# Rank rows read back in pair layout inside the experts' stage, with shared rows and residual summed in its loop

## The reference, cut to what matters

```python
h = layer_norm(ALPHA * x + merged @ prm['w_out'], prm['ln1_g'], prm['ln1_b'], LN_EPS)
y = layer_norm(ALPHA * h + moe_ffn(h, prm), prm['ln2_g'], prm['ln2_b'], LN_EPS)
# moe_ffn: each token goes to TOP_K = 8 of N_EXPERTS = 128 experts, and to one shared expert
h = jax.nn.silu(xb @ prm['w_e1'][e]) * (xb @ prm['w_e3'][e])
yb = (h @ prm['w_e2'][e]).astype(jnp.float32) * w[:, None]
shared = (jax.nn.silu(xt @ prm['w_s1']) * (xt @ prm['w_s3'])) @ prm['w_s2']
return (shared.astype(jnp.float32) + routed).astype(x.dtype).reshape(B, T, D)
```

## Time and profile before

| what | value |
|---|---|
| median of 3 runs | 2015.7 us (2013.69 to 2016.78) |
| profiled execution | 2011.83 us, its span 2010.1 us |
| experts' loop | about 870 to 1940 us of the span |
| combining stage | about 1941.4 to 2010.1 us |
| TensorE (PE) busy | 1785.3 us, 89% |
| VectorE, ScalarE, GpSimd busy | 632.4, 392.4, 363.7 us |
| bytes moved | 532.04 MB |

### The profile page before, as it was taken

How to read it: one execution, slowest core, us unless ns; L and a number is a source line. 1 busy time by engine, 2 the same in 40 slices (tenths; PEclk the granted TensorE clock), 3 DMA queues, 4 the chain that set the end, 5 groups by cost and what they waited for, 6 DMA issues and landing times. The chain is left out here.

```text
span 2010.1 us, 29270 instructions
## 1 busy us (share of the span) xinstructions
PE 1785.3 (89%) x10614; PEld 1052.4 (52%) x10614; DVE 632.4 (31%) x1516; ACT 392.4 (20%) x918; POOL 363.7 (18%) x529
## 2 busy tenths in 40 slices
PE   8999996889999999989988979888888888888877
PEld 6857765877778885555433333333333333333332
DVE  1387755774204312521111111111111111111127
ACT  0115544442120101311111111111111111111103
POOL 1000001888870000011111111111111111111100
PEclk8999998999999999999998989989898989989998
DMA  4443312011243434369999999999999999999976
GB/s 118 146 139 105 105 32 48 3 34 27 56 147 87 126 89 179 139 258 418 422 420 417 412 418 398 421 413 402 410 398 408 408 410 405 397 412 409 408 287 254
DMA packets 160782, 532.04 MB, mean 265 GB/s; under 512 B 22061, under 2 KB 88927, under 8 KB 110205
## 3 DMA queue, kind: packets, MB, share of 16 engines
q1 hardware_dynamic: 138971, 488.63, 61.8%
q0 software_dynamic: 20640, 41.23, 5.5%
q10 hardware_dynamic: 1098, 1.18, 0.2%
HBM read 522.52 MB, written 41.42 MB: 281 GB/s over the span
## 5 line engine op out<-in xcount | busy, mean ns | idle before, releaser
L1937 PE MATMUL bank<-arena 128*64 128x512 f32 x2048 | 511.9, 658 | 141.2 <-DMA arena<-in_w_e 139.8
L1937 PEld LDWEIGHTS bank<-arena 128*64 128x64 f32 x2048 | 158.9, 151 | 489.9 <-issue 488.4
L1955 PE MATMUL bank<-arena 128*64 128x512 f32 x1024 | 233.8, 599 | 0.0
L2177 DVE TENSOR_TENSOR arena<-bank,arena 128x256 f32<-128x256 f32 x64 | 27.2, 425 | 579.6 <-ACT arena L2022 579.6
L1805 POOL DMA_INDIRECT arena<-h_rows,index x66 | 67.1, 1017 | 776.0 <-DVE index L2051 715.3
L1425 PE MATMUL bank<-arena 128*128 128x276 f32 x768 | 184.7, 399 | 7.3 <-ACT arena L1527 3.1
L1425 PEld LDWEIGHTS bank<-arena 128*128 128x128 f32 x768 | 146.4, 191 | 41.7 <-ACT arena L1527 3.5
L1201 PE MATMUL bank<-arena 64*64 64x64 f32 (+2 forms) x2816 | 125.2, 244 | 28.8 <-DVE arena L1314 14.3
L2022 ACT ACTIVATE arena<-bank 128x256 f32<-128x256 f32 x64 | 24.7, 386 | 605.1 <-PE bank L1937 605.1
L1201 PEld LDWEIGHTS bank<-arena 64*64 64x64 f32 x2816 | 110.7, 140 | 35.2 <-DVE arena L1314 15.5
L1955 PEld LDWEIGHTS bank<-arena 128*64 128x64 f32 x1024 | 67.8, 136 | 110.9 <-issue 109.7
(11 more groups left out here) (333 smaller groups left out, 1842.8 us busy)
## 6 DMA issues: line engine op xcount, KB each, us to landing
arena<-in_w_e SPq DMA_DIRECT2D x384, 1024.0 KB
arena<-in_w_in SPq DMA_DIRECT2D x50, 512.0 KB, 4.2
arena<-routed_rows SPq DMA_DIRECT2D x8, 2048.0 KB, 23.4
arena<-in_w_mem_kv SPq DMA_DIRECT2D x4, 1024.0 KB, 5.8
arena<-in_cache_mem_k SPq DMA_DIRECT2D x8, 512.0 KB, 4.6
arena<-in_cache_mem_v SPq DMA_DIRECT2D x8, 512.0 KB, 5.8
arena<-in_w_out SPq DMA_DIRECT2D x2, 2048.0 KB, 12.3
arena<-in_w_s SPq DMA_DIRECT2D x3, 1024.0 KB, 10.5
```

The costliest lines, as they stand in the source:

```text
L1937: mm = pe.matmul(p_gu[t * S:(t + 1) * S, :], xt[:, v, c, t * S:(t + 1) * S], w13[2 * v + t][:, :, c, :], start=(c == 0), stop=(c == KD - 1))
L1955: mm = pe.matmul(p_y[h][t * S:(t + 1) * S, :], hidT[:, j, t * S:(t + 1) * S], w2[2 * v + t][:, j, h * 512:(h + 1) * 512], start=(j == 0), ...
```

## The change

The combining stage is gone, and its work is in the experts' stage.

- `w2s` is loaded ahead of the loop. In pairs 12 to 21 (TensorE's i from 6 to 10), `base` forms, for one tile and one half of the columns, the shared rows plus ALPHA times `h` in bank 7: two matmuls of 512 columns and four of 128 (with `alpha`, the identity times ALPHA). VectorE copies each to `res`. The residual rows aren't loaded any more.
- The ranks of a prompt tile are read by four loads of 1 MB, two for the low ranks (0 to 3) and two for the high. Each takes 64 tokens; partition x*64 + t gets ranks 2x and 2x+1 (of its four) of token t, 8 KB in one piece. The source is walked as [2, 64, 2048] elements, the destination as [128, 2048].
- The loads of low ranks begin when the scatter of pair 61 has landed (no token has one of its low ranks above expert 123). The fourth waits for the scatter of pair 62. The high ranks wait for that of pair 63. The samples' ranks come with one load of 1 MB, its source walked as [8, 16, 2048].
- TensorE adds two ranks at a time with `m.fold` (two 64 x 64 identity matrices above each other), 8 matmuls on 64 array columns for the four low or high ranks of a tile, and 4 matmuls with `fold32` for the samples. VectorE has no ranks to add. The layer norm is that of `mean` and `norm`, one tile after the other, in the order `LAST`.

```diff
+O_ALPHA = O_W2S + 2 * D
+O_FOLD32 = O_ALPHA + P
...
+O_HSAM = O_SSIL
+assert O_HSAM + KD * BS * TS <= O_YG
+O_CSTAT, O_CJUNK = O_PLACE, O_INFO
+PART = 2 * D
+O_LOW = ((O_HT, O_HT + PART), (O_WEXP[0], O_WEXP[0] + PART), (O_WEXP[1], O_WEXP[1] + PART),
+         (O_WEXP[0] + 2 * PART, O_WEXP[1] + 2 * PART))
+O_HIGH = ((O_WEXP[2], O_WEXP[2] + PART), (O_WEXP[3], O_WEXP[3] + PART), (O_WEXP[2] + 2 * PART, O_WEXP[3] + 2 * PART), (O_XG, O_XTE))
+O_SPART = O_W2S
+assert O_HT + 2 * PART <= O_INFO
+RES_ROWS = [P] * (NTT - 1) + [BS * TS]
+LAST = (0, 1, 2, NTT - 1, 3)
...
+        sp.wait_ge(s_oh, 1)
+        sp.dma_start(w2s, io["w_s2"][0].rearrange("(k p) n -> p k n", p=P)).then_inc(sem("shared_down_loaded"), 16)
...
-        res, w2s = m.at(O_RES, NTT, D), m.at(O_W2S, 2, D)
-        for i, (c0, n) in enumerate(TILES[:-1]):
-            sp.dma_start(res[:, i, :], io["h_rows"][c0:c0 + n, :]).then_inc(sem("h_rows_back"), 16)
-        for t in range(TS):
-            sp.dma_start(res[t:BS * TS:TS, NTT - 1, :], io["h_rows"][SEQ + 1 + t:NT:SB, :]).then_inc(sem("h_rows_back"), 16)
-        sp.dma_start(w2s, io["w_s2"][0].rearrange("(k p) n -> p k n", p=P)).then_inc(sem("shared_down_loaded"), 16)
+        routed = io["routed_rows"].rearrange("(t k) d -> t k d", k=TOPK)
+        def ranks(i, place, first, s):
+            for a in range(2):
+                t0 = TILES[i][0] + a * HD
+                sp.dma_start(m.arena[:, place[i][a]:place[i][a] + PART],
+                             routed[t0:t0 + HD, first:first + 4, :].rearrange("t (x k) d -> x t (k d)", x=2)).then_inc(s[i], 16)
+        def low(i):
+            ranks(i, O_LOW, 0, s_low)
+        def high(i):
+            ranks(i, O_HIGH, 4, s_high)
+        sp.wait_ge(s_base, 2 * NTT + 13)
+        sp.wait_ge(s_out[1], (16 * NP // 2) * count)
+        low(0)
+        sp.wait_ge(s_xt, NP * count)
+        low(1)
+        low(2)
+        sp.wait_ge(s_out[0], (16 * NP // 2) * count + 16)
+        low(3)
+        sp.wait_ge(s_out[1], (16 * NP // 2) * count + 16)
+        for i in range(3):
+            high(i)
+        sp.wait_ge(s_xt, NP * count + 1)
+        sp.dma_start(spart, io["routed_rows"][SEQ * TOPK:NT * TOPK].rearrange("(b y k) d -> b y (k d)", b=BS, k=2)[:, 4:4 * SB])              .then_inc(sem("sample_ranks_loaded"), 16)
+        sp.wait_ge(s_in[1], (16 * NP // 2) * count + 16)
+        high(3)
+        for g, i in enumerate(LAST):
+            c0, n = TILES[i]
+            sp.wait_ge(s_y_out, g + 1)
+            if i < NTT - 1:
+                sp.dma_start(io["out_y_p"][0, c0:c0 + n, :], res[:, i, :]).then_inc(sem("outputs_written"), 16)
...
+        def base(t, h):
+            n, cols = RES_ROWS[t], slice(t * P, (t + 1) * P)
+            bank = m.ps[7][0:n, :]
+            for j in range(2):
+                pe.matmul(bank, sact[:, j, cols] if n == P else ssam[:, j, :], w2s[:, j, h * 512:(h + 1) * 512],
+                          start=(j == 0), stop=False)
+            for k in range(4):
+                mm = pe.matmul(bank[:, k * P:(k + 1) * P], hT[:, 4 * h + k, cols] if n == P else hsam[:, 4 * h + k, :], alpha,
+                               start=False, stop=(k == 3))
+            mm.then_inc(s_bp, 1)
+        def fold(i, place, s):
+            high = place is O_HIGH
+            pe.wait_ge(s[i], 32)
+            for h in range(2):
+                for k in range(2):
+                    for a in range(2):
+                        part = m.at(place[i][a], PART)
+                        mm = pe.matmul(final_bank(i, h)[a * HD:(a + 1) * HD, :], m.fold[:, :],
+                                       part[:, k * D + h * 512:k * D + (h + 1) * 512],
+                                       start=(not high and k == 0), stop=(high and k == 1))
+            if high:
+                mm.then_inc(s_all, 1)
...
+        pe.wait_ge(sem("shared_down_loaded"), 16)
+        pe.sem_inc(s_bp, 12)
...
+                        with pe.If(i > 5):
+                            pe.wait_ge(s_base, 2 * i + (v + 1))
+                            for t in range(NTT):
+                                with pe.If(i < 7 + t):
+                                    with pe.If(i > 5 + t):
+                                        base(t, v)
+        pe.wait_ge(s_idx, NP * count + 3)
+        pe.wait_ge(s_xt, NP * count + 1)
+        pe.wait_ge(s_hc, NP * count)
+        pe.wait_ge(s_yv, NP * count + 1)
+        pe.wait_ge(s_ya, NP * count + 1)
+        for i in range(NTT - 1):
+            fold(i, O_LOW, s_low)
+        for i in range(3):
+            fold(i, O_HIGH, s_high)
+        pe.wait_ge(s_fmean, 1)
+        pe.wait_ge(sem("sample_ranks_loaded"), 16)
+        for h in range(2):
+            for k in range(2):
+                mm = pe.matmul(final_bank(NTT - 1, h)[0:BS * TS, :], fold32,
+                               spart[:, k * D + h * 512:k * D + (h + 1) * 512], start=(k == 0), stop=(k == 1))
+        mm.then_inc(s_all, 1)
+        fold(3, O_HIGH, s_high)
...
+        for g, i in enumerate(LAST):
+            n, st = RES_ROWS[i], fstats[0:RES_ROWS[i], i, :]
+            act.wait_ge(s_fmean, g + 1)
+            act.activation(fjunk[0:n, :], res[0:n, i, :], ACT.Square, bias=st[:, 3:4], accum_out=st[:, 4:5]).then_inc(s_fsq, 1)
+            act.wait_ge(s_fvar, g + 1)
+            act.activation(st[:, 6:7], st[:, 5:6], ACT.Sqrt).then_inc(s_fdev, 1)
...
+            for k in range(KD):
+                last = dve.tensor_copy(hsam[:, k, :].rearrange("p (b t) -> p b t", b=BS), sample_cols(hT[:, k, SEQ:NT]))
+            last.then_inc(s_base, 13)
+        dve.tensor_scalar(alpha, m.ident[:, :], ALPHA, None, ALU.mult)
+        dve.tensor_reduce(fold32, m.ident[:, :].rearrange("p (n x) -> p n x", x=4), AX.X, ALU.add)
...
+                        with dve.If(i > 2):
+                            dve.wait_ge(s_bp, 4 * i + (u + 1))
+                            dve.tensor_copy(m.arena[:, ds(2 * D * i + (O_RES - 6 * D + 512 * u), 512)], m.ps[7][:, :])\
+                               .then_inc(s_base, 1)
...
+        def final_mean(g, i):
+            n, st, zi = RES_ROWS[i], fstats[0:RES_ROWS[i], i, :], res[0:RES_ROWS[i], i, :]
+            dve.wait_ge(s_all, g + 1)
+            for h in range(2):
+                cols = slice(h * 512, (h + 1) * 512)
+                dve.scalar_tensor_tensor(out=zi[:, cols], in0=zi[:, cols], scalar=1.0, in1=final_bank(i, h)[0:n, :],
+                                         op0=ALU.mult, op1=ALU.add, accum_out=st[:, h:h + 1])
+            dve.drain()
+            dve.tensor_tensor(st[:, 2:3], st[:, 0:1], st[:, 1:2], ALU.add)
+            dve.drain()
+            dve.tensor_scalar(st[:, 3:4], st[:, 2:3], -1.0 / D, None, ALU.mult).then_inc(s_fmean, 1)
+        def final_norm(g, i):
+            n, st, zi = RES_ROWS[i], fstats[0:RES_ROWS[i], i, :], res[0:RES_ROWS[i], i, :]
+            dve.wait_ge(s_fsq, g + 1)
+            dve.tensor_scalar(st[:, 5:6], st[:, 4:5], 1.0 / D, LN_EPS, ALU.mult, ALU.add).then_inc(s_fvar, 1)
+            dve.scalar_tensor_tensor(out=zi, in0=zi, scalar=st[:, 3:4], in1=lnp[0:n, 0, :], op0=ALU.add, op1=ALU.mult)
+            dve.wait_ge(s_fdev, g + 1)
+            dve.reciprocal(st[:, 7:8], st[:, 6:7])
+            dve.drain()
+            dve.scalar_tensor_tensor(out=zi, in0=zi, scalar=st[:, 7:8], in1=lnp[0:n, 1, :], op0=ALU.mult, op1=ALU.add)\
+               .then_inc(s_y_out, 1)
+        dve.wait_ge(sem("ln2_loaded"), 32)
+        for g, i in enumerate(LAST):
+            final_mean(g, i)
+            final_norm(g, i)
...
-STAGES = (stage_load, stage_front, stage_wkv_to_experts, stage_combine)
+STAGES = (stage_load, stage_front, stage_wkv_to_experts)
```

More of the change, by code:

```diff
@@ L1679 @@
 O_W2S = O_RES + NTT * D
-assert O_W2S + 2 * D <= O_PLACE
+O_ALPHA = O_W2S + 2 * D
+O_FOLD32 = O_ALPHA + P
+assert O_FOLD32 + BS * TS <= O_PLACE
+O_HSAM = O_SSIL
[9 more added lines that the diff above has]
+LAST = (0, 1, 2, NTT - 1, 3)
 ABSENT = 4096.0
@@ L1723, in mix_programs @@
     s_rounds = sem("rounds_known")
+    res, w2s, spart = m.at(O_RES, NTT, D), m.at(O_W2S, 2, D), m.at(O_SPART, PART)
+    alpha, fold32, hsam = m.at(O_ALPHA, P), m.at(O_FOLD32, BS * TS), m.at(O_HSAM, KD, BS * TS)
+    fstats, fjunk = m.at(O_CSTAT, NTT, 8), m.at(O_CJUNK, D)
+    s_bp, s_base = sem("base_product"), sem("base_copied")
+    s_low = [sem(f"low_ranks_loaded_{i}") for i in range(NTT - 1)]
+    s_high = [sem(f"high_ranks_loaded_{i}") for i in range(NTT - 1)]
+    s_all, s_fmean, s_fsq = sem("ranks_added"), sem("final_mean"), sem("final_squares")
+    s_fvar, s_fdev, s_y_out = sem("final_variance"), sem("final_deviation"), sem("final_rows")
     S = SLOTS
@@ L1730, in z_bank, with final_bank @@
         return m.ps[2 * (i % 2) + h][at:at + n, :]
+    def final_bank(i, h):
+        return m.ps[2 * (i % 4) + h]
     def rounds(eng):
@@ L1766, in sync @@
                     load(r, NP - 2 + v, v, 2 * v)
-        res, w2s = m.at(O_RES, NTT, D), m.at(O_W2S, 2, D)
-        for i, (c0, n) in enumerate(TILES[:-1]):
```

(38 more changed lines are left out.)

105 lines of the change are left out of this document (removed).

## The result

The changed kernel takes a median of 2268.25 us (2267.79 to 2272.55, four runs) against 2014.7 us (2009.72 to 2016.78) for the kernel before: ratio 1.1268, interval 1.125 to 1.1286. It is slower by 12.7%. All medians and ratios leave out two executions at a much lower granted clock: one of the kernel before at 3001.78 us, and one of `e4_norms_woven` at 2266.7 us. The profiled execution took 2267.79 us, with a span of 2266.0 us.

What follows compares the result with a forecast made beforehand. The experts' loop was taken as bound by weight loads. Start of rank loads at 1917.1, plus loads 316.5 and 5.1, landing, fold, norm, output and 1 for the start gave 2255.5, on the median 2261.1 us; range 2235 to 2300.

Steps and rivals of the forecast that it cites:

- two fixed engines: Likeliest case for the rank loads: every load runs on one same pair of DMA engines, 2261.1 us, chance 0.84.
- Two engines, the same two for all loads: Rank loads: the source's outer count of 2 caps the DMA engines, giving share 0.13 and 53 GB/s.
- The start of the low loads: Behind the last weights: the two engines start on low ranks at 1917.1, possibly 10 us later.
- The loads' own time: Rank loads: sixteen of 1.0486 MB at 53 GB/s take 316.5 us, the samples' load 5.1 us.
- The end: Behind the last ranks: landing 2 us, last fold 5.5, layer norm 5.9, output 2.4.
- `w2s` ahead of the loop: Loop start: its 1 MB shares the DMA engines with the first gather; 1 us taken, at most 2.5.
- `base` hidden in the loop: TensorE in ten pairs: 5.4 us of new work meets 7.4 us of cover, costing nothing; 27 us without cover.
- The last scatter in a busy queue: Scatter of pair 63: lands by 1945.3 even if it takes 8.2 us, so the queue never runs dry.
- The loop's end at about 1936: Last output product: stands where it stood; 10 us or more later would mean `base` or `w2s` was costed wrong.
- The sixteen engines' rival: Rank loads: all 16 DMA engines work on each load, so the change gains, 1995.6 us, chance 0.12.

Runs made afterwards that it cites:

- e4_norms_woven: The kernel of `e1_token_outer` with VectorE's final layer norm steps of two tiles interleaved: 1999.36 us, ratio 0.9918 to the kernel before.
- e2_outer_counts: The kernel before plus four 1 MB probe loads behind its outputs, source outer counts 16, 8, 4 and 2, each waited for: 2067.56 us, one execution.
- e1_token_outer: The changed kernel with rank loads' source walked token outermost, [64, 2, 2048], and the fold matrix matched: 2002.72 us, ratio 0.9941 to the kernel before.
- e7_low_after_scatter: The kernel of `e6_sample_spread` with the low rank loads issued behind the last scatter: 2009.35 us, ratio 0.9979 to the kernel before.
- e3_no_base: The kernel of `e1_token_outer` without the matmuls of `base`, so shared rows and residual are missing: 2001.3 us, ratio 0.9928 to the kernel before.
- e6_sample_spread: The kernel of `e4_norms_woven` with the samples' load walked [16, 8, 2048] instead of [8, 16, 2048]: 1991.28 us, ratio 0.9905 to the kernel before.

## Why the prediction was right

It said 2261.1 us, 2235 to 2300, with two fixed engines as the likeliest case; the measured median is 2268.25. Its sum ended at a span of 2255.5 us, and the span measured is 2266.0, so the error of the sum is 10.5 us. On the medians it looks like 7, since the profiled execution of before, from which the sum was made, lay 3.9 us under its median, and that of after did not: those 3 us are luck. Point by point:

- **Two engines, the same two for all loads: shown.** Share 0.13 and 53 GB/s for nearly 300 us, and `e2_outer_counts` and `e1_token_outer` show the outer count as the cause. By the Trainium skill, page "DMA: Bandwidth & Descriptors", section "Why a DMA increments its semaphore by 16 and not by 1", the slowest counts of both patterns set the split; the traces agree, now also for counts that differ: 2, 4, 8 and 16 against 128. That the engines are the lowest-numbered, as the same section has it, no run shows.
- **The start of the low loads: mis-sized by 10 us.** I let the two engines begin at 1917.1, when most engines are through with the weights. The folds say when they did: 1969.33 - 39.4 for the first two loads - 2 for the landing = 1927.9. The two that serve the rank loads are those that are last with the weights, which `e7_low_after_scatter` shows running on until about 1927 with no other load in the queue. That they are the same two is worked out from this start time; the trace has no numbers of engines. The prediction had this as a possible 10 us more and took the other value; that is the error of the sum, while the smaller ones cancel.
- **The loads' own time: right.** From the first fold to the last are 281.2 us, for 14 rank loads and what the samples' load adds: 14 x 19.8 + 5.1 = 282. The samples' load itself had its stretch near 2185 at half share, as forecast, but moved 172 GB/s there and not 207.
- **The end: nearly right.** The last fold took 6.55 us instead of 5.5; from its end to the output's issue are 5.9 us, as costed. From that issue to the end of the span are 3.0 us instead of 2.4.
- **`w2s` ahead of the loop: 0.5 us, not 1.** The wait grew from 4.87 to 5.41 us, and the first weight of the next pair is issued at 879.69 against 879.24. By the loop's end nothing is left of it.
- **`base` hidden in the loop: shown,** by the same issue of the last weights (1896.94) and by `e3_no_base`. The sum of 5.4 us of work against 7.4 of cover for two pairs came out closer than costed: five such sums would be 27 against 37, and 30.2 us of work left 11.0 idle. The clock that I counted as part of the cover did rise: the 180 us that stand above at 0.98 and 169.16 us of TensorE read so in the windows' view of the kernel before:

```profile
1060.00:1240.00 180.00, 150.63 (x707) 62.83 (x705) 29.52 (x82) 22.29 (x41) 21.54 (x22) 0.91 1.00 413
```

- **The last scatter in a busy queue: 8.2 us assumed,** 8.8 measured (1940.84 to 1949.65). It decides nothing here, since the low ranks last until far behind it.
- **The loop's end at about 1936: off by 3 us.** The last hidden product took 9.8 us instead of the 7.09 of before, at a clock of 0.50 (windows from 1922 to 1926) behind its wait of 3.89 us for the weights. It is hidden too.
- **The sixteen engines' rival,** 1995.6 us: `e1_token_outer` came to 2002.7 and `e6_sample_spread` to 1991.3. In `e1_token_outer` the first high tile's norm starts 21.5 us behind the loop's end, as in the rival's sum; then VectorE waits 3.8 us for the third high tile and 5.3 for the samples, which is the 9 us that the time behind the loop is longer. Both come from ranks that land late, in or behind the slow stretch of some 12 us in which the samples' load, in its form of eight outer steps, is in flight. That this load causes it is argued from the shorter and less deep stretch of `e6_sample_spread`, which also had the woven norms.

What stays open is why the same two engines are late with the weights, why an engine moves 16 GB/s in the probe's loads with 4, 8 and 16 outer steps and 26.5 in the one with two, and why loads of different patterns in flight together keep all engines busy and yet move only 137 to 311 GB/s.

## What to carry to other kernels

Read every load's source pattern for its slowest count: with 2 there, 1 MB takes 20 us on two engines, and with 64 it takes 2.5, for the same bytes in the same pieces; if partitions can be permuted (here a fold matrix absorbs it), put the long axis outermost. Where a few engines carry a load, ask first when these become free: they may be the ones that are last with the stage before. A gain from overlap (15 us here) was lost seventeen times over by the form of one kind of load.

## What the runs showed of the hardware that was not expected

- Issuing waits for the queue. In the kernel after, SyncE's first rank load is issued at 1912.98, and the fourteenth is through only 250 us later, 19.9 us for each from the third on (its issue starts at 1923.99); with 16 engines the fourteen take 35.24 us, waits for semaphores included. The outputs behind them wait too: the first tile's last step of the norm ends at 2138.7, and its output is issued at 2207.12.
- Full share is not full rate. With all engines busy, the rate was 421 GB/s for rank loads with 64 outer steps, 262 for 16 outer steps a megabyte apart, 137 to 164 while the samples' load with eight outer steps was in flight beside the high loads, and 249 while high loads with 64 outer steps ran beside low ones with two.
- Two engines end their part of the weights 10 us behind the other fourteen, with nothing else queued for them.
